# Attention of a hybrid diffusion step: maximum and exponent moved into the next unit, transposed groups set between score blocks

## What is computed

```python
def mla_attention(q_nope, q_rope, k_nope, k_rope, v):
    ...
    scale = (QK_NOPE + QK_ROPE) ** -0.5
    def block(qs):                       # one block of 128 queries
        qn, qr = qs
        s = jnp.einsum("bqhd,bkhd->bhqk", qn, k_nope) + jnp.einsum("bqhr,bkr->bhqk", qr, k_rope)
        p = jax.nn.softmax(s.astype(jnp.float32) * scale, axis=-1).astype(v.dtype)
        return jnp.einsum("bhqk,bkhd->bqhd", p, v)
```

## Time and profile before

| | before |
|---|---|
| time, median of 3 runs (lowest to highest) | 1840.47 us (1836.44 to 1841.76) |
| the profiled execution, its own time / its span | 1839.76 / 1837.9 us |
| TensorE busy, share of the span | 1693.5 us, 92% |
| VectorE busy / ScalarE busy | 1050.5 us, 57% / 714.7 us, 39% |
| granted TensorE clock, mean of the span | 0.971 |
| attention stretch, 540 to 860 us: TensorE busy / VectorE / ScalarE | 278.9 / 153.3 / 130.0 us of 320 |

### The profile page before, as it was taken

The page is one execution under the profiler, slowest core; times in us unless marked ns, Lnnn a source line. Parts: engine busy times, 40 slices in busy tenths (PEclk is TensorE's granted clock), DMA queues, the critical chain, the costliest instruction groups (busy, mean ns, idle before and its releaser), DMA issues. The chain is left out here.

```text
span 1837.9 us, 24603 instructions
## 1 busy us (share of the span) xinstructions
PE 1693.5 (92%) x9795; PEld 1509.6 (82%) x9795; DVE 1050.5 (57%) x1586; ACT 714.7 (39%) x1185; POOL 78.7 (4%) x116
## 2 busy tenths in 40 slices
PE   5799999989878989996997899999999999899997
PEld 5687888877667777775877899999999999788885
DVE  6645755328755444545556655555555555466787
ACT  5543322323344343434455433333333333434453
POOL 1000000004300000000000000000000000000000
PEclk8899999999989999998998999999999999999998
DMA  8433142001310000003431122222222223673345
GB/s 307 137 100 130 65 161 100 25 32 46 92 42 18 1 13 1 1 1 128 170 113 37 69 92 78 97 96 97 96 76 87 90 90 126 225 231 111 122 133 202
DMA packets 96641, 176.32 MB, mean 96 GB/s; under 512 B 10224, under 2 KB 51392, under 8 KB 96528
## 3 DMA queue, kind: packets, MB, share of 16 engines
q1 hardware_dynamic: 92432, 169.75, 27.2%
q0 software_dynamic: 4096, 5.01, 0.9%
HBM read 131.02 MB, written 43.70 MB: 95 GB/s over the span
## 5 line engine op out<-in xcount | busy, mean ns | idle before, releaser
L421 PE MATMUL psF<-gv,gu_ring 128*128 128x320 f32 x1232 | 384.7, 312 | 14.9 <-DVE gv L2318 5.3
L422 PE MATMUL psF<-gv,gu_ring 128*128 128x320 f32 x1232 | 383.8, 312 | 0.0
L423 PE MATMUL psF<-gv,gu_ring 128*128 128x320 f32 x1232 | 383.7, 311 | 0.0
L421 PEld LDWEIGHTS psF<-gv,gu_ring 128*128 128x128 f32 x1232 | 234.1, 190 | 16.2 <-issue 11.9
L422 PEld LDWEIGHTS psF<-gv,gu_ring 128*128 128x128 f32 x1232 | 234.4, 190 | 0.0
L423 PEld LDWEIGHTS psF<-gv,gu_ring 128*128 128x128 f32 x1232 | 234.0, 190 | 0.0
L421 PE MATMUL psF<-d_w_ring,d_hid_ring 128*128 128x512 f32 x360 | 141.8, 394 | 4.9 <-DVE d_w_ring L2407 4.9
L422 PE MATMUL psF<-d_w_ring,d_hid_ring 128*128 128x512 f32 x360 | 141.3, 392 | 0.0
L423 PE MATMUL psF<-d_w_ring,d_hid_ring 128*128 128x512 f32 x360 | 141.1, 392 | 0.0
L421 PE MATMUL psP<-hT_hi,win_hi 128*128 128x512 f32 (+1 forms) x336 | 120.5, 359 | 0.7 <-DVEq L1028 0.7
L423 PE MATMUL psP<-hT_hi,win_lo 128*128 128x512 f32 (+1 forms) x336 | 119.2, 355 | 0.0
(11 more groups left out here) (385 smaller groups left out, 3633.9 us busy)
## 6 DMA issues: line engine op xcount, KB each, us to landing
hid_variants<-hraw SPq DMA_DIRECT2D x77, 320.0 KB, 2.2
d_hid<-hid_variants SPq DMA_DIRECT2D x77, 320.0 KB, 3.0
m_wring<-in_w_mod SPq DMA_DIRECT2D x24, 1024.0 KB, 6.8
d_b<-in_w_down SPq DMA_DIRECT2D x44, 256.0 KB, 3.6
win_raw<-in_w_in SPq DMA_DIRECT2D x18, 512.0 KB, 4.5
raw_gu<-in_w_gate SPq DMA_DIRECT2D x11, 512.0 KB, 4.1
raw_gu<-in_w_up SPq DMA_DIRECT2D x11, 512.0 KB, 4.8
hraw<-in_w_gate SPq DMA_DIRECT2D x11, 512.0 KB, 3.8
```

Source lines behind the costliest of these rows:

```text
L421: pe.matmul(out, w_hi, x_hi, start=first, stop=False, skip_group_check=onto)
L422: pe.matmul(out, w_hi, x_lo, start=False, stop=False, skip_group_check=onto)
L423: return pe.matmul(out, w_lo, x_hi, start=False, stop=last, skip_group_check=onto)
```

## The change

Three engines get a new order inside the loop over t; the instructions themselves stay the same.

```diff
@@ scalar
-            def pt(u):
+            def pt(u, only=None):
...
-                    if t % 2 == 0 and t >= 4:
-                        out(u // 2 - 2)
+                    if t >= 3:
+                        pt(u - 3, 2)
+                    if t % 2 == 1:
+                        if t >= 3:
+                            pt(u - 2, 0)
+                        exp(u - 1)
+                    else:
+                        if t >= 2:
+                            exp(u - 1)
+                        if t >= 4:
+                            out(u // 2 - 2)
+                        if t >= 2:
+                            pt(u - 2, 0)
                     if t >= 2:
-                        pt(u - 2)
-                    exp(u)
+                        pt(u - 2, 1)
                     if t == 5 and h + 1 < HEADS:
                         split(h + 1)
+                pt(u - 2, 2)
+                exp(u)
@@ vector
-                    if t >= 2:
-                        pt(u - 2, 0)
+                    if t >= 1:
+                        maximum(u - 1)
+                    if t >= 3:
+                        pt(u - 3, 2)
                     if t % 2 == 0 and t >= 4:
                         out(u // 2 - 2)
-                    maximum(u)
                     if t >= 2:
-                        pt(u - 2, 1)
+                        pt(u - 2, 0, 2)
                     if t >= 1:
                         invert(u - 1)
                     if t == 5 and h + 1 < HEADS:
                         split(h + 1)
+                maximum(u)
+                pt(u - 2, 2)
@@ tensor
-                    scores(u, 0)
+                    n = len(pieces(u))
                     if t % 2 == 0 and t >= 4:
                         values(u // 2 - 2, 1)
                     if t >= 2:
                         transposes(u - 2, 0)
-                    scores(u, 1)
+                    for i in range(n - 1):
+                        scores(u, i)
                     if t >= 2:
                         transposes(u - 2, 1)
+                    scores(u, n - 1)
+                    if t >= 2:
+                        transposes(u - 2, 2)
                     if t >= 3 and t % 2 == 1:
                         values(u // 2 - 1, 0)
```

More of the change, by code:

```diff
@@ L1508, in pt @@
                 for i, g in enumerate(groups(units[u][1])):
+                    if only not in (None, i):
+                        continue
                     act.wait_ge(pt_done, g0 + i + 1)
@@ L1597, in out, with pt @@
                                   ).then_inc(o_read, 1)
-            def pt(u, part):
+            def pt(u, first=0, last=3):
                 g0, r = n_groups(u), (u % 2) * P
                 for i, g in enumerate(groups(units[u][1])):
-                    if (i >= 2) == bool(part):
+                    if first <= i < last:
                         dve.wait_ge(pth_ready, g0 + i + 1)
@@ L1639, in _ @@
                 out(u // 2 - 1)
-                for part in range(2):
-                    pt(u - 1, part)
+                pt(u - 1)
                 if h + 1 < HEADS:
                     low(h + 1, "k")
-                for part in range(2):
-                    pt(u, part)
+                pt(u)
                 if h + 1 < HEADS:
@@ L1683, in project, with scores @@
                     mm.then_inc(proj, 1)
[L1685 to L1690, removed]
+            def scores(u, piece):
+                t = units[u][1]
+                last = piece == len(pieces(u)) - 1
+                late = last and not (len(pieces(u)) == 1 and u % 2 == 0)
                 if u == 0:
                     pe.wait_ge(in_lo, len(landed))
-                if u % NT == 0 and part == 0:
+                if u % NT == 0 and piece == 0:
                     pe.wait_ge(drained, n_proj(units[u][0] + 1))
-                elif u % NT >= 1 + (part == 0):
-                    pe.wait_ge(e_ready, u - 1 + part)
+                elif u % NT >= 1 + (not late):
+                    pe.wait_ge(e_ready, u - 1 + late)
                 q = slice(t * P, (t + 1) * P)
-                for col, k0, w in todo:
+                for col, k0, w in pieces(u)[piece:piece + 1]:
                     out, ks = S[:, col:col + w], slice(k0, k0 + w)
@@ L1705, in scores, with transposes @@
                     mm = pe.matmul(out, qr[:, q], L.kr_lo[:, ks], start=False, stop=True)
-                    if (col, k0, w) == pieces(u)[-1]:
+                    if last:
                         mm.then_inc(score, 1)
-            def transposes(u, part):
+            def transposes(u, group=None):
                 g0 = n_groups(u)
@@ L1713, in transposes @@
                 for i, g in enumerate(groups(units[u][1])):
-                    if (i >= 2) != bool(part):
+                    if group not in (None, i):
                         continue
@@ L1765, in _ @@
                 values(u // 2 - 1, 1)
-                for part in range(2):
-                    transposes(u - 1, part)
+                transposes(u - 1)
                 if h + 1 < HEADS:
                     project(h + 1, "k")
-                for part in range(2):
-                    transposes(u, part)
+                transposes(u)
                 if h + 1 < HEADS:
```

## The result

| | before | changed |
|---|---|---|
| median (lowest to highest) | 1840.14 us (1836.44 to 1841.76, 4 runs) | 1853.07 us (1852.29 to 1853.14, 4 runs) |
| span of the profiled run | 1837.9 us | 1851.3 us |
| ratio to before | | 1.0072 (95% interval 1.0055 to 1.009) |

The change costs 12.9 us, 0.7%. The forecast was 1855.6 us, range 1845 to 1868.

What follows compares the result with a forecast made beforehand. TensorE was taken to set the pace, with 12.07 us of work in a 13.91 us pair. Waits of +10.0 us plus clock falls of +5.1 gave +15.1 on the median 1840.5: 1855.6 us, range 1845 to 1868.

Steps and rivals of the forecast that it cites:

- T0 of an odd unit: TensorE's first transpose group of odd 128-query units waits for the buffer of the previous unit's second group: 0.91 us.
- V1: Late value product of a unit pair waits for a low half queued behind the maximum: 1.30 us, thrice a head.
- V1 behind the split: Weight split in heads 0 to 2 delays V1 by 1.79 us, to 3.09; another 0.60 in head 1.
- The pair: TensorE's closed loop over two units without a split: 14.40 us against 13.91 before, +0.49.
- The wait of S' for the exponent: The last, 256-wide score piece's 0.5 us wait was to go, except in a head's first three units.
- Those before T2: Waits before a unit's last, two-tile transpose group, 0.6 to 0.7 us twice a pair, were to go.
- The sum: Four heads' waits: 2.8+3.4+2.8+1.0 = +10.0 us; with the clock's charge +15.1 us.
- The clock: Clock at half behind the long wait in heads 0 to 2: 1.7 us three times, +5.1 us.
- The first rival: Same waits, but the clock stays up: +10.0 us, 1850.5 us; chance 0.20.
- the second: Clock falls also behind the plain V1 waits: nine more falls at 1.7, +15.3, 1871 us; chance 0.13.
- The third rival: Faster: VectorE reaches V1's low half sooner, maximum earlier or overlapped; all waits gone, split hidden: 1829 us; chance 0.09.
- The fourth rival: Within 0.3%: waits half as long as counted and no clock fall, +5, 1845.5 us or less; chance 0.11.

Runs made afterwards that it cites:

- e3: Changed kernel with ten extra, thrown-away 512-wide score matmuls before V1 at t = 6 of heads 0 to 2: 1848.1 us, ratio 1.0041.
- e1: Changed kernel with the next head's weight split moved to turn 6, behind the exponent (ScalarE) and the last group's low half (VectorE): 1842.9 us.
- e2: Changed kernel with two VectorE calls swapped, the last group's low half ahead of the maximum: 1835.7 us, ratio 0.9971.
- e5: Changed kernel with the call swap of e2 and the later weight split of e1 together: 1832.3 us, ratio 0.9958.
- e7: Changed kernel with the first transpose group of odd units moved behind the first 512-wide score piece: 1847.2 us, ratio 1.0038.
- e6: e5 with the first score piece ahead of V1 or an odd unit's first transposes, and early value product ahead of the last score piece: 1837.4 us.
- e9: Kernel before with the changed order on VectorE and ScalarE only, TensorE's order as before: 1852.6 us, ratio 1.0073.
- e10: e5 with the edit of e7, odd units' first transpose group behind the first score piece: 1834.8 us, ratio 0.9967.
- e8: e6 with ScalarE's weight split ahead of the exponent in turn 6 and the only score piece ahead of V1 at t = 8: 1831.1 us.
- e4: Kernel before with TensorE's new order alone: 1843.7 us, ratio 1.0019.

## Why the prediction was right

**The added waits** are all there and of the size given. T0 of an odd unit: 0.91 us forecast, 0.75 of idle plus 0.16 measured. V1: 1.30 forecast, 1.21 plus 0.16 measured, at t = 4, 6 and 8 (1.15 at the first of all). V1 behind the split: 3.09 forecast, 3.03 plus 0.16; with the third part 3.69 and 3.63 plus 0.16. The pair: 14.40 and 14.44 us.

**The removed waits.** The wait of S' for the exponent went inside the pairs (8 waits are left in the changed kernel, at t = 1 and at t = 9). I had said that it would be left in the first three units only; at t = 2 S' came just in time and t = 9 has one of 0.29. Those before T2 went inside the pairs and stayed at t = 2 and 8.

**The sum.** By heads I gave 2.8, 3.4, 2.8 and 1.0 for the waits and 1.7 three times for the clock: 4.5, 5.1, 4.5, 1.0. Measured 4.3, 5.9, 4.5, 1.1. Three heads agree within 0.2 us. Head 1 is 0.8 over the forecast, since the clock was down for 6.9 us there instead of 3.4 (V1 to T1 took 7.81 us, 2.4 more than the 5.44 of a plain one; in heads 0 and 2 1.5 and 1.6 more). So the heads give 15.7 us where I forecast 15.1, and the medians 12.9: the 2.3 us outside the heads went the other way. How near the total came, 1853.1 against 1855.6, says less than the heads do.

**The clock** was the least certain term, charged from one row of another stage. e3 measured it by itself, 5.7 us against the 5.1 charged. That is partly luck: in heads 0 and 2 the fall cost a little less than the 1.7 charged (1.5 and 1.6), in head 1, where it lasted twice as long, more (2.4). The first rival, clock up, falls with it, and the second, that the plain waits bring the clock down, falls with the traces of the changed kernel and of e1: plain waits at V1 and a steady clock of 1.00 side by side. The Trainium skill's sentence on power scaling (Perfetto Trace Analysis, Matmul Optimizations) agrees in kind with the rows and with e3.

**The third rival,** faster, named the right place and the wrong reason: nothing overlaps the maximum, but two calls swapped (e2) turn the sign. I wrote that V1's wait must fall by 0.84 us for the change to come out even; that was counted on the average head, split included. Without the split I had a head at +1.0, and e1's four heads stand at +1.0 to +1.1. Where all of V1's waits and the split's delay go, I had a head at -2.9. That case is e5: its heads 0 and 2 are 2.1 us under the kernel before, and TensorE's wait for the exponent, which I left out of that case, grew from 5.0 us in the changed kernel to 7.7. The fourth rival, waits half as long, falls with the waits above, which came in full. The rule of the Trainium skill that ScalarE's and VectorE's queues are strictly first in, first out (PSUM — Partial Sum Buffer, Engine vs sequencer instructions) agrees with the trace of the changed kernel: the low half at 577.47 had its copy ready for 2.8 us and started only when the maximum from 575.87 was through.

What I got wrong lies behind the prediction: e7 (a second chain not followed), e6 (a free place in a queue taken for free in another order) and e9 (a pair charged at twice what it cost). e5 and e10 came out above their ranges by 1.3 and 1.8 us.

## What to carry to other kernels

When an operation is moved up in an engine's queue, ask what it now stands in front of, and who waits for that. Here a 1.6 us maximum moved ahead of a 0.4 us subtraction, and the matmuls waited for the subtraction. Odd jobs that were hidden in an idle stretch, such as the next head's weight split, have to be placed anew each time the order around them changes. Before a change to a software pipeline is made, write down each closed loop (here the buffer ring with 2.16 us, and the maximum with the exponent, 1.70 us up to the exponent's start) and the place of every wait in it; a step taken out of one loop is worth only its distance to the next.

## What the runs showed of the hardware

The clock also fell without a long wait. In e2 it went to half at the end of head 2, behind four short waits in a row, and not at the end of heads 0, 1 and 3 with the same waits. TensorE's rows, then windows over the ends of heads 2, 0 and 1:

```profile
759.47 0.41 PE L1733 MATMUL psPT<-const,prob 128*128 128x128 f32 x2 [0.53 <-DVE pt_lo L1619]
...
760.06 0.63 PE L1733 MATMUL psPT<-const,prob 128*128 128x128 f32 x4 [0.19 <-DVE pt_lo L1619]
...
760.96 0.63 PE L1733 MATMUL psPT<-const,prob 128*128 128x128 f32 x4 [0.27 <-DVE pt_lo L1619]
...
761.99 0.39 PE L1714 MATMUL psScore<-kn_hi,q_hi 128*128 128x256 f32 x1 [0.40 <-ACT prob L1501]
...
760.00:766.00 6.00, 5.27 (x28) 4.85 (x29) 3.37 (x9) 2.83 (x8) 0.00 (x0) 0.72 0.00 0
593.00:599.00 6.00, 4.62 (x34) 3.75 (x33) 4.46 (x12) 3.36 (x9) 0.00 (x0) 1.00 0.01 3
672.00:678.00 6.00, 4.80 (x33) 4.04 (x34) 4.04 (x12) 2.96 (x8) 0.00 (x0) 1.00 0.00 1
```

The profiled runs of e5, e6, e8, e9 and e10 have one to three such falls in the heads; the kernel before, e1, e3 and e4 have none. All eleven falls, e2's included, stand at the same place of a head, behind the short waits at its end, and each lasts 3.4 us. The changed kernel's own short waits there (0.53, 0.19, 0.28 and 0.29 us in head 0) brought none. A long wait isn't certain to bring one either: in e7 V1 waits 2.52 us in heads 0 and 2 alike, and the clock fell in head 0 alone. Why the same waits bring it down in one head and not in the next stays open, and I made no run for it. By e3 a fall of 3.4 us costs 1.5 to 1.6 us, so one to three are 1.5 to 4.8 us, and my estimate is that 0.1 to 0.3% of such an order's time can't be forecast from its waits alone.
